# First operands of a down projection: another place in SBUF, and loads in another order

## The reference

```python
def sq_relu_mlp(h, w_up, w_down):
    return jnp.square(jax.nn.relu(h @ w_up)) @ w_down
...
x = x + rmsnorm(sq_relu_mlp(rmsnorm(x, g_mlp_pre), w_up, w_down), g_mlp_post)
```

## Time and profile before

| | us |
|---|---|
| median of three runs (lowest, highest) | 2822.18 (2820.95, 2823.1) |
| the profiled execution, its own time | 2823.11 |
| its span | 2821.6 |
| PE busy with matmuls | 2762.3 (98%) |
| DVE busy | 2122.2 (75%) |
| ACT busy | 1117.5 (40%) |
| POOL busy | 275.8 (10%) |
| mean granted TensorE clock | 0.992 of full |

### The profile page before, as it was taken

One profiled execution on the slowest core, in us unless ns is written; L12 is line 12 of the kernel. 1 busy time (PEld: TensorE's weight loads), 2 busy tenths in 40 slices (PEclk: granted clock), 3 DMA queues, 4 the chain that ended last, 5 costly groups with the idle time before them and its releaser, 6 DMA issues.

```text
span 2821.6 us, 48166 instructions
## 1 busy us (share of the span) xinstructions
PE 2762.3 (98%) x18594; PEld 2537.7 (90%) x18594; DVE 2122.2 (75%) x2695; ACT 1117.5 (40%) x1416; POOL 275.8 (10%) x444
## 2 busy tenths in 40 slices
PE   7999999999999999898999999999999999999998
PEld 6999999899899999767999999999978888888887
DVE  6788887665566653757877777777789888888886
ACT  8143333333333323444544444444443333333332
POOL 0000002233312100000000000000010000000000
PEclk9999999999999999999999999999999999999999
DMA  6444436556757553432344444444454443545353
GB/s 237 141 124 131 122 115 206 174 188 193 238 178 234 189 196 120 120 105 92 118 148 146 146 140 146 146 140 146 146 188 144 147 124 118 158 127 160 94 180 135
DMA packets 387960, 430.37 MB, mean 153 GB/s; under 512 B 13879, under 2 KB 300845, under 8 KB 385645
## 3 DMA queue, kind: packets, MB, share of 16 engines
q1 hardware_dynamic: 346088, 269.19, 31.8%
q0 software_dynamic: 41504, 159.26, 16.3%
q10 hardware_dynamic: 228, 0.06, 0.0%
HBM read 342.21 MB, written 86.25 MB: 152 GB/s over the span
## 4 chain that ended last, share of the span: by engine, by line
PE 85%; DVE 7%; issue 3%; DMA 2%; ACT 2%; DVEq 0%; POOL 0%; SPq 0%; ACTq 0%; POOLq 0%
PE gemm L2929 23%; PE aux L3026 5%; PE aux L3028 5%; PE aux L3027 5%; PE gemm L3026 5%; PE gemm L3028 5%; PE gemm L3027 5%; PE gemm L3614 3%; PE gemm L3615 3%; PE gemm L3616 3%; PE aux L3616 3%; PE aux L3614 3%; PE aux L3615 3%; PE aux L3072 2%; PE aux L3625 1%
## 5 line engine op out<-in xcount | busy, mean ns | idle before, releaser
L2929 PE MATMUL gemm<-act_hi,w_hi 128*128 128x288 f32 x1744 | 390.9, 306 | 4.5 <-DVE act_lo L2396 3.3
L2929 PE MATMUL gemm<-act_hi,w_lo 128*128 128x288 f32 x1744 | 374.0, 296 | 0.0
L2929 PE MATMUL gemm<-act_lo,w_hi 128*128 128x288 f32 x1744 | 373.5, 296 | 0.0
L2929 PEld LDWEIGHTS gemm<-act_hi,w_hi 128*128 128x128 f32 x1744 | 279.4, 189 | 32.9 <-issue 22.1
L2929 PEld LDWEIGHTS gemm<-act_hi,w_lo 128*128 128x128 f32 x1744 | 281.3, 189 | 0.0
L2929 PEld LDWEIGHTS gemm<-act_lo,w_hi 128*128 128x128 f32 x1744 | 281.2, 189 | 0.0
L1697 ACT ACTIVATE w_hi<-w_raw 128x2048 fp32r<-128x2048 f32 x60 | 115.2, 1920 | 302.4 <-PE aux L3616 173.5
L2580 DVE TENSOR_TENSOR w_lo<-w_raw,w_hi 128x1024 fp32r<-128x1024 f32 x120 | 146.7, 1223 | 108.3 <-ACT w_hi L1620 108.3
L1807 DVE TENSOR_TENSOR w_lo<-w_raw,w_hi 128x2048 fp32r<-128x2048 f32 x63 | 144.1, 2287 | 47.1 <-ACT w_hi L1199 46.8
L3026 PE MATMUL aux<-act_hi,w_hi 128*128 128x288 f32 x528 | 155.4, 294 | 0.0
L3028 PE MATMUL aux<-act_hi,w_lo 128*128 128x288 f32 x528 | 155.4, 294 | 0.0
(11 more groups left out here) (522 smaller groups left out, 7700.4 us busy)
## 6 DMA issues: line engine op xcount, KB each, us to landing
w_raw<-in_w_mlp_up SPq DMA_DIRECT2D x120, 512.0 KB, 4.1
w_raw<-in_w_mlp_down SPq DMA_DIRECT2D x32, 1024.0 KB, 6.2
side_hi<-in_w_mlp_down SPq DMA_DIRECT2D x32, 1024.0 KB, 7.1
w_raw<-in_w_in SPq DMA_DIRECT2D x29, 1024.0 KB, 6.7
w_raw<-in_w_in SPq DMA_DIRECT2D x54, 512.0 KB, 4.1
w_raw<-in_w_out SPq DMA_DIRECT2D x16, 1024.0 KB, 6.1
u_sum_scratch<-u_sum POOLq DMA_DIRECT2D x32, 512.0 KB, 2.9
z_scratch<-z_out SPq DMA_DIRECT2D x56, 288.0 KB, 2.4
```

The costliest lines, as they stand in the source:

```text
L2929: ins = M(out[half][:, 0:TH], w[b][:, cols], x[:, k, half * TH:(half + 1) * TH], start=first and n == 0, stop=last and n == 2)
```

## The change

- `u_op_early` is now 16 chunks of 576 columns, the shape of `x_op`, instead of 9 rows of 1024; each operand takes 256 columns of four chunks within one token half. Half 0 holds A11 and S1 (high and low parts), half 1 holds A12, `u_smp` and the high part of S2. The low part of S2 moves to a ninth row of `u_op_late`, in `act_lo`.
- POOL loads A11 and S1 of the first block when product 0 of the last pair is done, ahead of the last but one `v_store`; before, these two and As1 and A12 waited for product 2 and stood behind it. As1 and A12 still wait for product 2.
- S2, S4 and S3 of the first block are loaded one behind the other when product 5 is done. Before, S2 waited only for the copy of As1 and S4 and S3 for `w_low` of stripe 1.
- Each load of sample columns becomes two transfers of half the size, in all blocks; the counts of `s_uin` double.
- ACT rounds A11 before the copy `v_e1`, not behind it.
- The load of `g_row`, which lies on the first words of `u_op_early`, waits for product 3 of the last block, not product 1.

```diff
-        u_op_late = sb("u_op_late", [P, 8, 1024], F32R, alias)
+        u_op_late = sb("u_op_late", [P, 9, 1024], F32R, alias)
-        u_op_early = sb("u_op_early", [P, 9, 1024], F32R, st)
+        u_op_early = sb("u_op_early", [P, KC, T], F32R, st)
...
-        u_op = {"S1": (u_slot(u_op_early, 0), u_slot(u_op_early, 1)), "A11": (u_slot(u_op_early, 2), u_slot(u_op_early, 3)),
-                "A12": (u_slot(u_op_early, 4), u_slot(u_op_early, 5)), "S2": (u_slot(u_op_early, 7), u_slot(u_op_early, 8)),
+        def u_side(t, n):
+            return u_op_early[:, 4 * n:4 * (n + 1), TH * t:TH * t + TP // 2]
+
+        u_op = {"S1": (u_side(0, 0), u_side(0, 1)), "A11": (u_side(0, 2), u_side(0, 3)),
+                "A12": (u_side(1, 1), u_side(1, 3)), "S2": (u_side(1, 0), u_slot(u_op_late, 8)),
...
-        u_smp = u_op_early[:, 6, :].rearrange("p (c t) -> p c t", c=FC)
+        u_smp = u_side(1, 2).rearrange("p k (c t) -> p k c t", c=2)
...
                 if name[1] == "s":
                     half = int(name[2]) - 1
-                    dst, src, done = u_smp[:, 4 * half:4 * half + 4, TS:2 * TS], u_v[f, half, :, :, TP:T], s_uin
+                    for i in range(2):
+                        pool.dma_start(u_smp[:, 2 * half + i, :, TS:2 * TS].bitcast(F32),
+                                       u_v[f, half, :, 2 * i:2 * i + 2, TP:T]).then_inc(s_uin, 16)
+                    return
...
             pool.wait_ge(s_usst, 16 * (U_GROUPS - 3))
+            pool.wait_ge(v_m, 7 * ALL_PAIRS - 6)
+            u_load(0, "A11")
+            u_load(0, "S1")
             v_store(pair(UP_PAIRS - 2))
             pool.wait_ge(v_m, 7 * ALL_PAIRS - 4)
-            for name in ("A11", "As1", "S1", "A12"):
-                u_load(0, name)
+            u_load(0, "As1")
+            u_load(0, "A12")
             s_store(pair(UP_PAIRS - 2))
             pool.wait_ge(u_h, u_count(0, "As1"))
             u_load(0, "As2")
+            pool.wait_ge(v_m, 7 * ALL_PAIRS - 1)
             u_load(0, "S2")
-            pool.wait_ge(s_wlo, w_count(0, 0, 1))
             u_load(0, "S4")
             u_load(0, "S3")
...
-            pool.wait_ge(s_tile, q_count(FB - 1, 0, Q_DONE[1]))
+            pool.wait_ge(s_tile, q_count(FB - 1, 0, Q_DONE[3]))
             pool.dma_start(g_row[:], g_mlp_post.to_broadcast([P, D])).then_inc(s_grow, 16)
...
             w_high(0, 0, 0, 0)
+            u_high(0, "A11")
             v_copy(pair(UP_PAIRS), v_e1, A[0], 7 * ALL_PAIRS - 2, 6 * ALL_PAIRS - 5)
-            u_high(0, "A11")
             u_high(0, "S1")
```

More of the change, by code:

```diff
@@ L448, in u_slot, with u_smp_chunk, u_smp_parts @@
             return region[:, n, :].rearrange("p (k t) -> p k t", k=4)
-        u_op = {"S1": (u_slot(u_op_early, 0), u_slot(u_op_early, 1)), "A11": (u_slot(u_op_early, 2), u_slot(u_op_early, 3)),
-                "A12": (u_slot(u_op_early, 4), u_slot(u_op_early, 5)), "S2": (u_slot(u_op_early, 7), u_slot(u_op_early, 8)),
+        def u_side(t, n):
+            return u_op_early[:, 4 * n:4 * (n + 1), TH * t:TH * t + TP // 2]
+        u_op = {"S1": (u_side(0, 0), u_side(0, 1)), "A11": (u_side(0, 2), u_side(0, 3)),
+                "A12": (u_side(1, 1), u_side(1, 3)), "S2": (u_side(1, 0), u_slot(u_op_late, 8)),
                 "A21": (u_slot(u_op_late, 0), u_slot(u_op_late, 1)), "A22": (u_slot(u_op_late, 2), u_slot(u_op_late, 3)),
                 "S4": (u_slot(u_op_late, 4), u_slot(u_op_late, 5)), "S3": (u_slot(u_op_late, 6), u_slot(u_op_late, 7))}
-        u_smp = u_op_early[:, 6, :].rearrange("p (c t) -> p c t", c=FC)
+        u_smp = u_side(1, 2).rearrange("p k (c t) -> p k c t", c=2)
+        def u_smp_chunk(c):
+            return u_smp[:, c // 2, c % 2, :]
+        def u_smp_parts(half):
+            two = u_smp[:, 2 * half:2 * half + 2]
+            return two[:, :, :, 0:TS], two[:, :, :, TS:2 * TS]
         side_flat = side_hi[:, :, :].rearrange("p k t -> p (k t)")
@@ L1669, in u_high @@
                 if name[1] == "s" or name == "A21":
-                    act.wait_ge(s_uin, f * 32 + {"As1": 16, "As2": 32, "A21": 48}[name])
+                    act.wait_ge(s_uin, f * 64 + {"As1": 32, "As2": 64, "A21": 80}[name])
                 else:
@@ L1673, in u_high @@
                 if name[1] == "s":
-                    rows = slice(4 * (int(name[2]) - 1), 4 * int(name[2]))
-                    dst, src = u_smp[:, rows, 0:TS], u_smp[:, rows, TS:2 * TS]
+                    dst, src = u_smp_parts(int(name[2]) - 1)
                 else:
@@ L2663, in u_low @@
                 if name[1] == "s":
-                    rows = slice(4 * (int(name[2]) - 1), 4 * int(name[2]))
-                    high, low = u_smp[:, rows, 0:TS], u_smp[:, rows, TS:2 * TS]
+                    high, low = u_smp_parts(int(name[2]) - 1)
                 else:
@@ L3622, in q_product @@
                         for k in range(4):
-                            both, cols = u_smp[:, 4 * sample + k, :], slice(k * 512, (k + 1) * 512)
+                            both, cols = u_smp_chunk(4 * sample + k), slice(k * 512, (k + 1) * 512)
                             M(bank[:], both, dw_hi[n][:, cols], start=o < 2 and k == 0, stop=False, skip_group_check=True)
@@ L3649, in last_stripe @@
                         else:
-                            both = u_smp[:, c, :]
+                            both = u_smp_chunk(c)
                             M(y_bank[t][:], both, dw_hi[n][:, cols], start=c == 0, stop=False, skip_group_check=True)
```

## The result

The changed kernel takes **2825.4 us** (2823.4 to 2829.4 over 22 runs), the kernel before 2822.2 (2820.3 to 2824.3 over 22). The ratio is 1.0012, 95% interval [1.0007, 1.0018]: slower by a little, where 4.3 us less were forecast. The forecast range ended at 2820.9.

A forecast was written before the change was run, and what follows sets the result against it. PE, 98% busy, bounds the kernel, but DVE's chain sets the first block's end. `w_high` of stripe 1 moving 4.3 us earlier, all else adding nothing, takes the median from 2822.18 to 2817.9 us, range 2816.0 to 2820.9.

The forecast's parts named there:

- The seam: Where up and down projections meet: PE's 2.55 us wait goes and `w_high` of stripe 1 starts 4.3 us earlier.
- As1 and d21: Loads for the first down-projection block: As1 taken to land after 5.6 us, weight load d21 after 8.3, costing nothing.
- the signs of being wrong: ACT waiting for As1 or d21; DVE idle before stripe 2's `w_low` or T2; weight loads over 200 ns; later waits gone.
- The spare of 0.1 us: At `w_high` of stripe 2 in the first block: weight load d21 lands with 0.1 us to spare.
- DMA engines taking turns: Rival, loads behind product 5: engines alternate between queues, d21 lands 0.4 us late; gain 3.9, 2818.3 us; chance 0.12.
- loads in order of issue: Argument against alternating queues, from the earlier trace: four small loads behind d12 took 8 to 9 us, not mixed.
- Operands in four pieces of 256 … nothing: The split operand layout in `u_op_early`: costs nothing, as DVE takes 1224 ns over a split tile, 1223 packed.
- PE weight loads from the split operands: Rival, down projection: 1,920 matmuls slow, each ns costing 1.9 us; 2833.3 us at 8 ns; chance 0.05.
- It would have to grow by over 40 ns to show: Argument against slower PE weight loads: a load takes 188 ns within a matmul pitch of 228.
- Each load still reads 128 words in a row: Argument against slower PE weight loads: the split layout leaves each load's 128 words contiguous; no size given.

The follow-up runs named there:

- e1: The changed kernel with token half 1's operands at columns 320 to 575 instead of 288 to 543; 2816.8 us, repeats 2818.8 and 2817.4.
- e8: The kernel before with a 64-byte pad behind the first two weight pairs, moving the third pair and all operand regions; 2831.9 us, ratio 1.0037.
- e5: The kernel before with a 64-byte pad ahead of the first weight buffer, moving all weight buffers and operand regions together; 2820.1 us, ratio 0.9994.
- e2: The changed kernel with token half 0's operands at columns 32 to 287 instead of 0 to 255; 2828.6 us, ratio 1.0027.
- e3: The changed kernel with token half 1's operands at columns 304 to 559 instead of 288 to 543; 2821.2 us, ratio 0.9999.
- e4: The kernel before with only the slots of `u_op_late` beginning 128 bytes later; 2830.4 us, ratio 1.0033.
- e7: The changed kernel with separate columns per operand pair, at distances 16, 96, 176, 240 and 0 bytes from the weight tile; 2824.2 us, one run.

## Why the prediction was wrong, point by point

- *The seam*: right in each step. PE waits no more, the clock doesn't fall, `w_high` of stripe 1 is released by the copy and not by T1, DVE sets the first block's end, the waits at products 4 and 6 stay (0.48 and 1.33 us). The gain is 4.3 us by the trace; e1, which is the change without its loss, has 2.5 to 4.2, and its 2816.8, 2818.8 and 2817.4 us stand around the forecast 2817.9.
- *As1 and d21*: As1 was there when ACT reached it. ACT waited 1.37 us for d21, from the issue at 2057.80 to 2065.49, 7.7 us where 8.3 were taken. It cost nothing: DVE had no idle in front of `w_low` of stripe 2 or T2, though a wait for d21 stood among the signs of being wrong. The spare of 0.1 us that the prediction gave d21 was none: 2070.13 - 4.3 + 2.0 is 2067.8, not 2068.0. The lower end of its range, 2816.0, is 0.7 below what its terms give, 2817.9 - 1.2. Neither slip bears on the miss.
- *DMA engines taking turns*: this gave 8.8 us for d21 and would have cost 0.4. d21 took 7.7, so the cost didn't come. But the reading against it, loads in order of issue, fails too. In the changed kernel d21 and d22, then (on the other queue) S2, S4 and S3, with the landings of each group (least, median, longest):

```profile
2057.80 0.92 SPq L885 DMA_DIRECT2D side_hi<-in_w_mlp_down  x2
DMA to landing us min/median/max: 7.7/10.7/13.7
2058.01 2.23 POOL L1162 DMA_DIRECT2D u_op_late<-u_sum_scratch  x3
DMA to landing us min/median/max: 9.2/10.7/12.2
```

  d22, issued at 2058.27, took 13.7 us where 12.6 were taken and landed at 2071.9, while S4, issued behind it, had landed at 2069.5 and S3 at 2071.7. So the loads of the two queues overlapped. T2 read d22 at 2072.29, 0.4 us later: that load was the close one, not d21.
- *"Operands in four pieces of 256 … nothing"*: **this step failed.** It costed the split layout by DVE alone, 1224 against 1223 ns, which is right for DVE. PE reads the operands too, and the layout put those in token half 1 128 bytes off the grid of the weight tiles: 6 ns on each of 80 matmuls a side, and 8.0 us in all.
- *The rival "PE weight loads from the split operands"*: the one that came true, at a chance of 0.05. Its price per ns, 1.9 us over 1,920 matmuls, was of the right size, but only half 1 was hit, some 1,200, at 6 ns. Both reasons against it were wrong. "It would have to grow by over 40 ns to show": the load's record stayed at 188 ns, as the row below shows for samples, which all lie in half 1, and the matmuls behind it still came 6 ns later. The room behind a load in the records is no reserve. "Each load still reads 128 words in a row": true, and not what counts.

```profile
L3638 PEld LDWEIGHTS gemm<-w_hi,u_op_early x104: 187/188/188, 2111.5 to 2679.5; 128*128 128x128 f32 x104
```

- The trace of the kernel before had such a difference in it, in the up projection, where the streamed x is read by token halves. The starts of the products of one pair: half 0, half 0, half 1, half 0, packed, half 1, packed, and the next pair.

```profile
1483.41 0.30 PE L3026 MATMUL gemm<-x_op,w_hi 128*128 128x288 f32 x1
...
1486.57 0.29 PE L3026 MATMUL gemm<-act_hi,w_hi 128*128 128x288 f32 x1
...
1489.73 0.30 PE L3026 MATMUL gemm<-x_op,w_hi 128*128 128x288 f32 x1
...
1492.93 0.29 PE L3026 MATMUL gemm<-act_hi,w_hi 128*128 128x288 f32 x1
...
1496.09 0.29 PE L3026 MATMUL gemm<-y_op,w_hi 128*128 128x288 f32 x1
...
1499.28 0.29 PE L3026 MATMUL gemm<-act_hi,w_hi 128*128 128x288 f32 x1
...
1502.48 0.30 PE L3026 MATMUL gemm<-y_op,w_hi 128*128 128x288 f32 x1
...
1505.68 0.30 PE L3026 MATMUL aux<-x_op,w_hi 128*128 128x288 f32 x1
```

24 matmuls each: 3.16, 3.16, **3.20**, 3.16, 3.19, **3.20**, 3.20 us. The third and the sixth stream token half 1, 1152 bytes into the row; the packed halves of `y_op` have rows of 1152 bytes, so that every second row is off too. As medians over 28 pairs that is 131.7 ns a matmul in half 0 and 133.3 to 133.4 in half 1. That the distance alone makes it isn't shown: e8 changes the distances here and leaves both halves of `x_op` as they are. Who had asked whether all matmuls of one shape run at one pace would have given this rival its due.

## What to carry to other kernels

Where PE is busy without a gap, cost a new operand layout by PE's own pace: take the time from one matmul's start to the next, by operand and by place, from the trace of before, not the duration of a record. Keep the operands that TensorE loads and streams side by side at one offset modulo 256 bytes, as measured here for fp32r operands against 512 columns; that needed the free 32 words of a half put in front of the operand and not behind it. And if a wait goes but the total doesn't follow, compare a stretch without waits in both traces first.

## What the runs showed of the hardware

- An fp32r matmul of 512 columns follows the one before after 226.7 ns if the operand being loaded and the one that streams lie a multiple of 256 bytes apart, and after 229 to 234 ns at 32, 64, 96, 128, 160, 176, 192 and 224 bytes; 16 and 240 bytes cost it only behind matmuls at another distance. Moving both together (e5) costs nothing; moving one off that grid (the changed kernel, e2 to e4, e8) does. It shows in neither the weight load's record (188 ns) nor the clock (1.00) nor a wait. The Trainium skill (SBUF — State Buffer, Specifications (TRN2)) gives cachelines of 16 bytes and asks for at least two hits in a line for full bandwidth. Every operand here begins at a multiple of 16 bytes and is read in a row, so by that rule none should be slower than another; the measurement decides.
- One slow distance slows matmuls behind it for a while: the samples in S4 of e4 (231.3 ns at distance 0), A11 in e7 (233 ns behind the samples, 227 ahead of them).
- Left open: why 176, 192 and 240 bytes cost less than 32 or 224, whether other types and widths behave so (the 288 columns of the up projection do in part, e8), and what in the chip meets at this distance. What e8 suggests for the up projection, weight tiles placed at the offset of the half that they meet, wasn't tried.
